# Gate rows and the rotary swap by transfers, the rotary products on GpSimd

## The chip, the cores and the metric

The kernel runs on one core of one Trainium2 chip. A core has TensorE (matrix products, PE in the profile), VectorE (DVE), ScalarE (ACT), GpSimd (POOL), SyncE (SP, which here only issues transfers) and 16 DMA engines. The metric is the time of one execution on the device in microseconds.

## The reference

Two blocks of two layers each run over 256 tokens of width 1024, in fp32. The first block takes its shifts, scales and gates from a vector `c` (adaLN): each of its four sublayers ends in `x + gate * y`. The second block begins with an attention that selects keys by an index score, and its queries, keys, index queries and index key get a rotary embedding.

```python
def first_block(x, c, ...):
    for i in range(DEPTH):
        mod = silu(c) @ ada_w[i] + ada_b[i]
        sh1, sc1, gt1, sh2, sc2, gt2 = jnp.split(mod, N_MOD, axis=-1)
        ...                                  # short convolution (i = 0) or RWKV-7 (i = 1)
        x = x + gt1[:, None, :] * y
        h = _modulate(_rmsnorm(x, norm_g[i, 1]), sh2, sc2)
        x = x + gt2[:, None, :] * (jnp.square(jax.nn.relu(h @ mlp_w1[i])) @ mlp_w2[i])
    return _rmsnorm(x, final_g)

def apply_rope(x):                           # per head of 64
    x1, x2 = x[..., :32], x[..., 32:]
    return jnp.concatenate([x1 * c - x2 * sn, x1 * sn + x2 * c], axis=-1)
```

## The kernel before

Every weight matrix is cut into units of 1 MB (256 columns of 1024 rows, or half of 512 columns). SyncE loads them in order into four `stage` buffers (`load_unit`, four units ahead). ScalarE makes the upper part `w_hi` of a unit, VectorE the rest `w_lo = stage - w_hi`, each in two halves (`split`), and TensorE multiplies three times (hi*hi, hi*lo, lo*hi) into a bank of PSUM (`unit`, `up_unit`, `wide_unit`). Each engine's program is written out by hand in its own order; semaphores tie them together. TensorE's order is the one that the others follow.

adaLN's modulation is summed piece by piece beside the convolution and the first MLP and ends as columns, `mods[layer][q, 8 * part + t]`, one value per partition. A gate is needed as a row, the same on all 128 partitions, since `y` is laid out with tokens on partitions. Before, `row_of_columns` (L2353) makes it on TensorE: eight products of a broadcast column with the identity, in two banks, and `row_copy` (L1039) on ScalarE copies both banks to `gate_rows[r]`. That happens four times: row 0 beside the convolution's unit 9, row 1 ahead of the first MLP's last wide units, row 2 in RWKV's output projection, row 3 behind it. Around row 3 TensorE also runs `unread`, a product of 512 columns that nobody reads, while VectorE computes the norm's scales. VectorE's `residual` (L1597 and following) multiplies by the row (L1611).

The rotary embedding goes in eight pieces: index key (128 channels), two of index queries, key, four of queries. For each, ScalarE copies the unit's bank to `rope_in` (`rope_load`, L1366); TensorE multiplies by a permutation matrix with signs (`rot`, L2781, `rot_query`, L2853), which swaps the halves of each head; VectorE multiplies the swapped one by `sin_root` (L2058); GpSimd multiplies the copy by `cos_root` (L850); VectorE adds them (L2060) and signals `rope_done`. `sin_root` and `cos_root` are the tables times the tokens' norm factors, made by VectorE (L2140, L2141). GpSimd takes the pieces strictly in order, each after the `rope_done` of the last, and between them makes the `w_lo` of three of the query units (L860). L2838 is the index scores, L2792 the logits of a pair of heads, L2803 and L2815 to L2819 the transposed shares and their products with the values. L1406 on ScalarE makes `k_dup`, the keys in both halves of the partitions.

The stage's order on TensorE is: units 0 and 1, `root_to_row`, then the swaps between units 2 to 8, with the index scores and the logits of the first pairs beside them.

Of the kernel before, what the change touches and what calls it, by code (L numbers as in the profile page):

```python
# [13 lines left out]
P = 128  # L14
SEQ = 256
# [33 lines left out]
CONST_PARTS = ((("ident", P), ("mean", P), ("ones", P), ("rot", P)),  # L49
# [13 lines left out]
def constant_table():  # L63
# [13 lines left out]
    rot = np.zeros((P, P))  # L77
    for m in range(P):
        d = m % HD
        rot[m + HD // 2 if d < HD // 2 else m - HD // 2, m] = -1.0 if d < HD // 2 else 1.0  # L80
    put("rot", rot)
# [11 lines left out]
    put("sin", np.tile(np.sin(ang), (4, 1)))  # L93
# [7 lines left out]
def build(nc, A, out):  # L101

    with ExitStack() as ctx:
# [65 lines left out]
        ident, mean_w, ones_w, head_ones, head_mean, rot_w = (c_(n) for n in ("ident", "mean", "ones", "head_ones", "head_mean", "rot"))  # L169
# [105 lines left out]
        rope_in = [at(f"rope_in{i}", [P, 2, SEQ], r_off[3] + 2048 * i) for i in range(2)]  # L275
        rope_c = at("rope_c", [P, 2, SEQ], r_off[3] + 4096)
# [285 lines left out]
        LAST_SET = ADA_SETS - 1  # L562

# [64 lines left out]
        def _(sp):  # L628
# [29 lines left out]

            for k in range(ADA_FIRST):
# [7 lines left out]
            for u in range(NU):  # L667
# [40 lines left out]
        row_done, row_out, out_made, final_made = (sem(n) for n in ("row_done", "row_out", "out_made", "final_made"))  # L708
# [18 lines left out]
        rot_done, rope_done, ki_copied, cos_done, kdup_ready = (sem(n) for n in ("rot_done", "rope_done", "ki_copied", "cos_done", "kdup_ready"))  # L727
# [9 lines left out]
        def _(pool):  # L737
# [135 lines left out]
        def _(act):  # L873
# [2161 lines left out]
```

## Time and profile before

| | us |
|---|---|
| median of 3 runs | 1352.4 (1350.19 to 1352.61) |
| profiled execution, its own time | 1350.53 |
| its span | 1348.8 |
| TensorE busy | 1303.3 |
| VectorE busy | 948.8 |
| ScalarE busy | 701.5 |
| GpSimd busy | 128.3 |

Times in the rows are microseconds from the start of the span. A product's record shows a modelled end that overlaps the next, so that the cost of one is read from start to start. An idle time in brackets is the engine's own just before, with what ended it. A releaser is inferred; where a wait has several semaphores, the name can be another's.

### The profile page before, as it was taken

The page shows a single profiled execution, that of the slowest core. Times are in us where ns is not written, and L with a number is a line of the kernel's source. Part 1 is how long each engine was busy: PE and PEld are TensorE (multiplying, and loading weights), DVE is VectorE, ACT ScalarE, POOL GpSimd, SP SyncE. Part 2 cuts the span into 40 slices and gives each one's busy share as a digit, 9 for nine tenths or more (in the row PEclk, how much of TensorE's full clock was granted, in tenths as well). Part 3 has the DMA queues.
Part 4 walks back from the last instruction along what each step waited for, and adds up shares of the span by engine and source line. Part 5 has one row for each costly group of instructions (what it writes and reads, how often), then busy time and mean ns, then how long its engine had stood idle before and what let it go on. Part 6 is the DMA issues. An engine that isn't in the chain of part 4 may idle for free. (4 is left out here: it accounts for less than half of the span.)

```text
span 1348.8 us, 24952 instructions
## 1 busy us (share of the span) xinstructions
PE 1303.3 (97%) x10507; PEld 1129.8 (84%) x10507; DVE 948.8 (70%) x1433; ACT 701.5 (52%) x1211; POOL 128.3 (10%) x133
## 2 busy tenths in 40 slices
PE   4999999999999999999999999999999999999997
PEld 2998888998899897788888887888888998888886
DVE  1887788976768776675566888666656677756655
ACT  2544544434567555564444648654445566644443
POOL 0000000010200764100000042000000021000000
PEclk9999999999999999999999999999999999999999
DMA  9996799995341012356665532465555543565561
GB/s 362 372 363 237 299 356 380 352 343 167 115 156 64 4 35 97 95 176 201 188 189 176 182 113 91 148 206 192 187 190 160 174 139 126 172 188 194 183 197 50
DMA packets 177575, 256.90 MB, mean 190 GB/s; under 512 B 10488, under 2 KB 122552, under 8 KB 177464
## 3 DMA queue, kind: packets, MB, share of 16 engines
q1 hardware_dynamic: 177464, 255.31, 56.8%
q8 instruction: 83, 1.36, 0.4%
q14 instruction: 28, 0.23, 0.1%
HBM read 254.25 MB, written 1.05 MB: 189 GB/s over the span
## 5 line engine op out<-in xcount | busy, mean ns | idle before, releaser
L1514 DVE TENSOR_TENSOR w_lo<-stage,w_hi 128x1024 fp32r<-128x1024 f32 (+1 forms) x372 | 447.6, 1239 | 160.4 <-ACT w_hi L889 160.0
L889 ACT ACTIVATE w_hi<-stage 128x1024 fp32r<-128x1024 f32 (+1 forms) x378 | 380.1, 1049 | 211.7 <-PE acc L2318 191.9
L2316 PE MATMUL acc<-w_hi,z_hi 128*128 128x512 f32 x640 | 252.6, 395 | 1.6 <-DVE z_lo L1963 1.6
L2318 PE MATMUL acc<-w_hi,z_lo 128*128 128x512 f32 x640 | 249.4, 390 | 0.0
L2317 PE MATMUL acc<-w_lo,z_hi 128*128 128x512 f32 x640 | 249.2, 389 | 0.0
L2259 PE MATMUL un<-h_both,w_hi 128*128 128x256 f32 x736 | 214.3, 291 | 1.8 <-POOL w_lo L860 1.1
L2260 PE MATMUL un<-h_both,w_hi 128*128 128x256 f32 x736 | 208.1, 283 | 0.0
L2261 PE MATMUL un<-h_both,w_lo 128*128 128x256 f32 x736 | 208.0, 283 | 0.0
L2259 PEld LDWEIGHTS un<-h_both,w_hi 128*128 128x128 f32 x736 | 140.8, 191 | 9.5 <-issue 5.4
L2316 PEld LDWEIGHTS acc<-w_hi,z_hi 128*128 128x128 f32 x640 | 120.1, 188 | 27.8 <-issue 4.0
L2260 PEld LDWEIGHTS un<-h_both,w_hi 128*128 128x128 f32 x736 | 141.0, 192 | 1.2 <-issue 0.7
L2318 PEld LDWEIGHTS acc<-w_hi,z_lo 128*128 128x128 f32 x640 | 120.1, 188 | 25.4
L2261 PEld LDWEIGHTS un<-h_both,w_lo 128*128 128x128 f32 x736 | 140.9, 191 | 0.0
L2317 PEld LDWEIGHTS acc<-w_lo,z_hi 128*128 128x128 f32 x640 | 120.3, 188 | 23.5
L2297 PE MATMUL un<-h_both,w_hi 128*128 128x512 f32 x384 | 121.2, 397 | 0.4 <-DVE w_lo L1514 0.4
L2297 PE MATMUL side<-h_both,w_hi 128*128 128x512 f32 x384 | 120.8, 396 | 0.4
L2300 PEld LDWEIGHTS side<-h_both,w_lo 128*128 128x128 f32 x384 | 72.1, 188 | 17.0
L2300 PEld LDWEIGHTS un<-h_both,w_lo 128*128 128x128 f32 x384 | 72.1, 188 | 16.9
L2300 PE MATMUL un<-h_both,w_lo 128*128 128x256 f32 x384 | 75.5, 278 | 0.0
L2300 PE MATMUL side<-h_both,w_lo 128*128 128x256 f32 x384 | 75.4, 278 | 0.0
L1796 DVE SCALAR_TENSOR_TENSOR ada_sum<-ada_buf,small,ada_sum 128x1024 f32<-128x1024 f32 x49 | 62.8, 1282 | 1.0
L2297 PEld LDWEIGHTS un<-h_both,w_hi 128*128 128x128 f32 x384 | 59.1, 189 | 1.6 <-DVE w_lo L1514 0.6
(393 smaller groups left out, 1886.0 us busy)
## 6 DMA issues: line engine op xcount, KB each, us to landing
stage<-in_mlp_w SPq DMA_DIRECT2D x64, 1024.0 KB
ada_buf<-in_ada_w SPq DMA_DIRECT2D x48, 1024.0 KB, 11.4
stage<-in_w_up SPq DMA_DIRECT2D x32, 1024.0 KB
stage<-in_w_down SPq DMA_DIRECT2D x32, 1024.0 KB
stage<-in_conv_w_in SPq DMA_DIRECT2D x12, 1024.0 KB
stage<-in_rw_w_rkv SPq DMA_DIRECT2D x12, 1024.0 KB
stage<-in_w_in_a SPq DMA_DIRECT2D x8, 1024.0 KB
stage<-in_w_kv_b SPq DMA_DIRECT2D x8, 1024.0 KB
```

What stands on the lines that cost most here:

```text
L889: A_(w_hi[u % 2][:, half, 0:n], stage[u % NSTAGE][:, half, 0:n], ACT.Copy).then_inc(hi_made, 1)
L1514: V.tensor_tensor(w_lo[u % 2][:, half, 0:n], stage[u % NSTAGE][:, half, 0:n], w_hi[u % 2][:, half, 0:n].bitcast(F32), ALU.subtract).then_i ...
L1796: V.scalar_tensor_tensor(out=to[:], in0=rows, scalar=by, in1=to[:], op0=ALU.mult, op1=ALU.add).then_inc(ada_weighed, 1)
L2259: MM(out, hi_l, hi_r, start=start, stop=False, skip_group_check=True)
L2260: MM(out, hi_l, lo_r, start=False, stop=False, skip_group_check=True)
L2261: return MM(out, lo_l, hi_r, start=False, stop=stop, skip_group_check=True)
L2297: MM(pair[:, m, :, :], wh[:, kt, c], h_both[:, kt, :, :], start=(kt == 0), stop=False, skip_group_check=True)
L2300: ins = MM(pair[:, m, 0, :], wl[:, kt, c], h_hi[:, kt, :], start=False, stop=(kt == KT - 1), skip_group_check=True)
L2316: MM(y, z_hi[:, kt, q], wh[:, i, :], start=(first and kt == 0), stop=False, skip_group_check=True)
L2317: MM(y, z_hi[:, kt, q], wl[:, i, :], start=False, stop=False, skip_group_check=True)
L2318: ins = MM(y, z_lo[:, kt, q], wh[:, i, :], start=False, stop=(last and kt == KT - 1), skip_group_check=True)
```

## The change

Gate rows: `row_of_columns` and `row_copy` are gone with their waits. SyncE writes the gate's columns to a buffer in memory (`keep_gate`) as soon as its order reaches unit 14, 32, 41 or 60, and reads them back as a row broadcast over the partitions (`spread_gate`) at unit 15, 33, 66 and, for the last, 68. `residual` waits for that transfer. In place of the fourth row's products TensorE runs four more `unread`s.

Rotary embedding: the swap matrix is gone, and its signs go into the sine table. ScalarE waits for its own copy to `rope_in` and issues four transfers, each of 32 partitions of `rope_in` to the neighbouring 32 of `rope_turned`. GpSimd multiplies by the cosine, waits for the four transfers, multiplies by the sine. VectorE only adds. TensorE's eight products are gone, and with them its waits for `rope_done` ahead of units 7 and 8.

```diff
-CONST_PARTS = ((("ident", P), ("mean", P), ("ones", P), ("rot", P)),
+CONST_PARTS = ((("ident", P), ("mean", P), ("ones", P), ("still", P)),
...
-    put("sin", np.tile(np.sin(ang), (4, 1)))
+    put("sin", np.tile(np.sin(ang), (4, 1)) * np.where(i % HD < HD // 2, -1.0, 1.0)[:, None])
...
         rope_in = [at(f"rope_in{i}", [P, 2, SEQ], r_off[3] + 2048 * i) for i in range(2)]
+        rope_turned = [at(f"rope_turned{i}", [P, 2, SEQ], tmp_off + 4096 + 2048 * i) for i in range(2)]
         rope_c = at("rope_c", [P, 2, SEQ], r_off[3] + 4096)
...
+        GATE_SETS = (2, 5, 8, 11)
+        KEEP_GATE_AT = (14, 32, 41, U_RWO)
+        SPREAD_GATE_AT = (15, 33, U_RWO + 6)
...
+            def keep_gate(r):
+
+                sp.wait_ge(ada_added, ADA_ORDER.index(GATE_SETS[r]) + 1)
+                c0 = 8 * (GATE_SETS[r] % 6)
+                sp.dma_start(gate_kept[r].rearrange("(t q) -> q t", q=P), mods[GATE_SETS[r] // 6][:, c0:c0 + KT],
+                             allow_slow_non_contiguous=True).then_inc(sem("gate_written"), 16)
+
+            def spread_gate(r):
+
+                sp.wait_ge(sem("gate_written"), 16 * (r + 1))
+                sp.dma_start(gate_rows[r][:], gate_kept[r].unsqueeze(0).to_broadcast([P, D])).then_inc(sem("gate_spread"), 16)
+
...
                     sp.dma_start(final_row[:], row_of(VEC_FINAL)).then_inc(sem("final_row_in"), 16)
+                    spread_gate(3)
...
+                if u in KEEP_GATE_AT:
+                    keep_gate(KEEP_GATE_AT.index(u))
+                if u in SPREAD_GATE_AT:
+                    if u == U_RWO + 6:
+                        sp.wait_ge(sem("bonus_gated"), len(GN_GROUPS))
+                    spread_gate(SPREAD_GATE_AT.index(u))
                 load_unit(u)
...
                 pool.wait_ge(un_free, freed(V_A + ROPE_USE[r]))
                 if r:
                     pool.wait_ge(sem("rope_done"), r)
-                G.tensor_tensor(rope_c[:, 0:n, :], rope_in[r % 2][:, 0:n, :], cos_root.unsqueeze(1).to_broadcast([P, n, SEQ]), ALU.mult)\
-                    .then_inc(sem("cos_done"), 1)
+                G.tensor_tensor(rope_c[:, 0:n, :], rope_in[r % 2][:, 0:n, :], cos_root.unsqueeze(1).to_broadcast([P, n, SEQ]), ALU.mult)
+                pool.wait_ge(sem(f"rope_landed{r % 2}"), 64 * (r // 2 + 1))
+                turned = rope_turned[r % 2][:, 0:n, :]
+                G.tensor_tensor(turned, turned, sin_root.unsqueeze(1).to_broadcast([P, n, SEQ]), ALU.mult).then_inc(sem("cos_done"), 1)
 
                 if r in (ROPE_K, ROPE_Q, ROPE_Q + 1):
...
-            def row_copy(r, low, high):
-
-                act.wait_ge(row_done, r + 1)
-                A_(gate_rows[r][:, 0:HALF], flat(low), ACT.Copy)
-                A_(gate_rows[r][:, HALF:D], flat(high), ACT.Copy).then_inc(row_out, 1)
-
...
                 copy_set(COPIED_AT.get(S_CONV + j))
-                if j == 9:
-                    row_copy(0, acc[0], acc[1])
...
             rw_split(3)
-            row_copy(2, stat_ps, misc)
             last_splits(U_RWO, N_MLP1)
             norm_split(N_MLP1, gain[:, 3, :], mods[1][:, 24:32], U_MLP[1] + 1)
-            row_copy(3, stat_ps, misc)
             mlp(1, N_A, vecT[:, VEC_GA:VEC_GA + KT])
 
...
                 if r >= 2:
                     act.wait_ge(rope_done, r - 1)
                 A_(rope_in[r % 2][:, 0:n, :], un[v % 2][:, 0:n, :], ACT.Copy, scale=scale).then_inc(un_free, 1)
+                act.wait_ge(un_free, freed(v))
+                for g in range(4):
+                    to, src = 32 * g, 32 * (g ^ 1)
+                    act.dma_start(rope_turned[r % 2][to:to + 32, 0:n, :], rope_in[r % 2][src:src + 32, 0:n, :]).then_inc(sem(f"rope_landed{r % 2}"), 16)
...
-                    dve.wait_ge(row_out, row + 1)
+                    dve.wait_ge(gate_spread, 16 * (row + 1))
                     link(V.tensor_tensor(g[:, k % 2, :], y, gate_rows[row][:, HALF * h:HALF * (h + 1)], ALU.mult))
                     y = g[:, k % 2, :]
...
-            def rope(r, n, dst, bank=misc):
-                dve.wait_ge(rot_done, r + 1)
-                link(V.tensor_tensor(dst, bank[:, 0:n, :], bc4(sin_root, n), ALU.mult))
+            def rope(r, n, dst):
                 dve.wait_ge(cos_done, r + 1)
-                V.tensor_tensor(dst, dst, rope_c[:, 0:n, :], ALU.add).then_inc(rope_done, 1)
+                V.tensor_tensor(dst, rope_turned[r % 2][:, 0:n, :], rope_c[:, 0:n, :], ALU.add).then_inc(rope_done, 1)
 
...
-            dve.wait_ge(rot_done, ROPE_KI + 1)
+            dve.wait_ge(wi_turned, 1)
...
-                rope(ROPE_Q + j, 2, q_fm[:, 2 * j:2 * j + 2, :], un[(V_A + 5 + j) % 2])
+                rope(ROPE_Q + j, 2, q_fm[:, 2 * j:2 * j + 2, :])
 
             rope_query(0)
             select(rounds - rounds // 2)
-            V.tensor_scalar(sel_bias[:], score[:], 0.5 * TAKEN, NEG, ALU.is_gt, ALU.mult).then_inc(sem("keys_chosen"), 1)
-            dve.wait_ge(sem("keys_chosen"), 1)
...
-            def row_of_columns(r, columns, low, high):
-
-                for t in range(KT):
-                    ins = MM(flat((low, high)[t // 4])[:, P * (t % 4):P * (t % 4) + P], columns[:, t:t + 1].to_broadcast([P, P]), ident,
-                             start=True, stop=True)
-                ins.then_inc(row_done, 1)
-
...
-                if tiles[0] == 0 and n == N_A:
-                    pe.wait_ge(row_out, 4)
...
-                            if m == 1 and g == 0 and j == 1:
-                                pe.wait_ge(row_out, 4)
                             up_unit(u + 2 * UPD * g + j, up_pair[j % 2], ready)
-                    if m == 0 and g == GROUPS - 1:
-                        pe.wait_ge(ada_added, LAST_SET)
-                        row_of_columns(1, mods[0][:, 40:48], stat_ps, misc)
                     if g == GROUPS - 1:
                         last_units(u + 2 * UPD * g + UPD, z_ready(zc + UPD * g), first=False, turn={1: N_A, 2: N_B}.get(m))
                         continue
...
-                if j == 9:
-                    pe.wait_ge(ada_added, 3)
-                    row_of_columns(0, mods[0][:, 16:24], acc[0], acc[1])
-            pe.wait_ge(row_out, 1)
             last_units(U_CONV_OUT, z_ready(Z_CONV))
...
-            row_of_columns(2, mods[1][:, 16:24], stat_ps, misc)
             wide_unit(U_RWO + 2, 1, rwo_ready, rows=range(0, 2))
             wide_unit(U_RWO + 2, 1, rwo_ready, rows=range(2, 4))
             wide_unit(U_RWO + 3, 3)
             keep_warm(V_MLP[1], 1)
-            pe.wait_ge(row_out, 3)
-            row_of_columns(3, mods[1][:, 40:48], stat_ps, misc)
-            unread(un[V_MLP[1] % 2], 2)
+            unread(un[V_MLP[1] % 2], 6)
             turn_first(N_MLP1)
...
-            def rot(r, n, v):
-                pe.wait_ge(un_free, freed(v))
-                if r:
-                    pe.wait_ge(rope_done, r)
-                MM(misc[:, 0:n, :], rot_w, rope_in[r % 2][:, 0:n, :], start=True, stop=True).then_inc(rot_done, 1)
...
-                if k >= 7:
-                    pe.wait_ge(rope_done, ROPE_Q + k - 6)
...
-            def rot_query(j):
-                v = V_A + 5 + j
-                pe.wait_ge(un_free, freed(v))
-                MM(un[v % 2][:], rot_w, rope_in[(ROPE_Q + j) % 2][:], start=True, stop=True).then_inc(rot_done, 1)
...
-                nc.tensor.transpose(misc[:, 1, IDX_HEADS * a:IDX_HEADS * (a + 1)], rope_in[ROPE_KI % 2][HD:KI_COLS, 0, P * a:P * a + P],
+                ins = nc.tensor.transpose(misc[:, 1, IDX_HEADS * a:IDX_HEADS * (a + 1)], rope_in[ROPE_KI % 2][HD:KI_COLS, 0, P * a:P * a + P],
                                     ident[HD:KI_COLS, HD:KI_COLS])
-            rot(ROPE_KI, 1, V_A)
+            ins.then_inc(wi_turned, 1)
             a_unit(2)
-            rot(ROPE_QI, 2, V_A + 1)
             a_half(3, 0)
-            rot(ROPE_QI + 1, 2, V_A + 2)
             a_half(3, 1)
             index_scores(0)
             a_half(4, 0, tokens=True)
-            rot(ROPE_K, 2, V_A + 3)
             index_scores(1)
             a_half(4, 1, tokens=True)
             a_unit(5)
-            rot_query(0)
             a_unit(6)
             pe.wait_ge(kdup_ready, KV_HEADS)
             pe.wait_ge(score_relu, QT * IDX_HEADS // 2)
             a_products(0)
             a_half(7, 0)
-            rot_query(1)
             a_products(1)
             a_half(7, 1)
             z_of = z_ready(Z_A)
...
                 if p == 1:
                     a_half(8, 0)
...
-                if p in (1, 3):
-                    rot_query(p // 2 + 2)
```

## Rows read from the trace of the kernel before

**Rows 1.** The page, busy time of each engine, share of span and instructions

```profile
PE 1303.3 (97%) x10507; PEld 1129.8 (84%) x10507; DVE 948.8 (70%) x1433; ACT 701.5 (52%) x1211; POOL 128.3 (10%) x133
```

**Rows 2.** Table by stretches: length, busy PE, PEld, DVE, ACT, POOL, granted clock, DMA

```profile
133.00:330.00 197.00, 196.31 (x1312) 173.14 (x1311) 158.31 (x171) 93.09 (x129) 6.29 (x3) 1.00 0.90 323
755.00:830.00 75.00, 71.17 (x562) 61.61 (x563) 63.64 (x149) 45.44 (x107) 27.64 (x32) 1.00 0.41 130
```

**Rows 3.** Timeline of PE around row 0 (start, length, what), and all of L2356

```profile
96.67 2.05 PE L2356 MATMUL acc<-const,mod 128*128 128x128 f32 x16
98.48 0.36 PE L2259 MATMUL un<-h_both,w_hi 128*128 128x256 f32 x1
...
L2356 PE MATMUL side<-const,mod x48: 270/275/275, 308.9 to 569.3; 128*128 128x128 f32 x48
```

**Rows 4.** Timeline of PE around row 2

```profile
552.38 1.95 PE L2356 MATMUL side<-const,mod 128*128 128x128 f32 x16
555.74 0.47 PE L2316 MATMUL acc<-w_hi,z_hi 128*128 128x512 f32 x1 [1.42 <-DVE z_lo L1963]
```

**Rows 5.** Timeline of PE around row 3 and the unread products

```profile
566.75 1.02 PE L2363 MATMUL un<-const 128*128 128x512 f32 x2
567.60 1.95 PE L2356 MATMUL side<-const,mod 128*128 128x128 f32 x16
569.38 1.88 PE L2363 MATMUL un<-const 128*128 128x512 f32 x4
571.55 1.09 PE L2326 MATMUL acc<-const,xs_sq 128*128 128x128 f32 x8 [0.29 <-DVE xs_sq L1537]
```

**Rows 6.** Issues by line: ns of an issue (min/median/max), us to landing

```profile
L681 SPq DMA_DIRECT2D lora_g2b<-in_rw_g x4: 417/421/429, 335.9 to 337.3; - x4
DMA to landing us min/median/max: 3.9/4.1/4.4
...
L672 SPq DMA_DIRECT2D lora<-in_rw_a x1: 4837/4837/4837, 163.3 to 163.3; - x1
...
DMA to landing us min/median/max: 2.0/2.1/2.1
```

The first landing line is L681's (32 KB each, behind other loads), the second L701's (the output, 256 KB each, nothing else in flight).

**Rows 7.** Timeline of SP's queue at units 14 and 15

```profile
97.46 0.39 SPq L644 DMA_DIRECT2D stage<-in_conv_w_out  x1
...
104.15 0.39 SPq L644 DMA_DIRECT2D stage<-in_conv_w_out  x1
```

**Rows 8.** Timeline of ACT in the rotary stage

```profile
763.23 1.99 ACT L889 ACTIVATE w_hi<-stage 128x1024 fp32r<-128x1024 f32 x2
...
825.69 0.58 ACT L1366 ACTIVATE rope_in<-un 128x512 f32<-128x512 f32 x1
```

**Rows 9.** Timeline of PE in the rotary stage

```profile
765.78 0.35 PE L2259 MATMUL un<-h_both,w_hi 128*128 128x256 f32 x1 [0.18 <-ACT rope_in L1366]
...
779.15 1.16 PE L2838 MATMUL acc<-ki_fm,qi_fm 64*128 64x128 f32 x16
...
828.96 0.93 PE L2792 MATMUL un<-k_dup,q_fm 64*128 64x128 f32 x8 [0.43 <-DVE q_fm L2060]
```

**Rows 10.** Timeline of DVE in the rotary stage

```profile
764.41 4.64 DVE L1514 TENSOR_TENSOR w_lo<-stage,w_hi 128x1024 fp32r<-128x1024 f32 x4 [0.42 <-ACT w_hi L889]
768.97 0.41 DVE L2140 TENSOR_TENSOR rstd<-const,acc 128x256 f32<-128x256 f32 x1
...
774.01 3.43 DVE L1514 TENSOR_TENSOR w_lo<-stage,w_hi 128x1024 fp32r<-128x1024 f32 x2
...
778.08 0.69 DVE L2060 TENSOR_TENSOR qi_fm<-qi_fm,rope_c 128x512 f32<-128x512 f32 x1
```

**Rows 11.** Timeline of POOL in the rotary stage

```profile
769.85 0.75 POOL L850 TENSOR_TENSOR rope_c<-rope_in,rstd 128x256 f32<-128x256 f32 x1 [219.98 <-DVE rstd L2141]
771.27 1.28 POOL L850 TENSOR_TENSOR rope_c<-rope_in,rstd 128x512 f32<-128x512 f32 x1 [0.67 <-DVE ki_fm L2060]
774.23 2.12 POOL L850 TENSOR_TENSOR rope_c<-rope_in,rstd 128x512 f32<-128x512 f32 x1 [1.68 <-DVE qi_fm L2060]
```

More of the change, by code:

```diff
@@ L76, in constant_table @@
     put("head_mean", same_head / HD)
[L77 to L81, printed above, removed]
     s, q = i[:, None] % CHUNK, np.arange(CHUNK)[None, :]
@@ L98, in constant_table, with build @@
     return t
-def build(nc, A, out):
+def build(nc, A, out, gate_kept):
     with ExitStack() as ctx:
@@ L167, in c_ @@
             return const[i][:, lo - CONST_AT[i]:hi - CONST_AT[i]]
-        ident, mean_w, ones_w, head_ones, head_mean, rot_w = (c_(n) for n in ("ident", "mean", "ones", "head_ones", "head_mean", "rot"))
+        ident, mean_w, ones_w, head_ones, head_mean = (c_(n) for n in ("ident", "mean", "ones", "head_ones", "head_mean"))
         level_t = c_("level_t").rearrange("p (j q) -> p j q", j=6)
@@ L707, in build @@
         xs_low_made, xs_high_made, turned, first_done = (sem(n) for n in ("xs_low_made", "xs_high_made", "turned", "first_done"))
-        row_done, row_out, out_made, final_made = (sem(n) for n in ("row_done", "row_out", "out_made", "final_made"))
+        gate_written, gate_spread, out_made, final_made = (sem(n) for n in ("gate_written", "gate_spread", "out_made", "final_made"))
         scaled_made, sq_f_ready, both_ready, square_ready, root_row_done, root_row_out, tables_made = (
@@ L726, in build @@
                              "bonus_gated", "weighed", "scaled", "group_done", "last_done"))
-        rot_done, rope_done, ki_copied, cos_done, kdup_ready = (sem(n) for n in ("rot_done", "rope_done", "ki_copied", "cos_done", "kdup_ready"))
+        wi_turned, rope_done, ki_copied, cos_done, kdup_ready = (sem(n) for n in ("wi_turned", "rope_done", "ki_copied", "cos_done", "kdup_ready"))
         score_done, score_relu, score_used = sem("score_done"), sem("score_relu"), sem("score_used")
@@ L1070, in mlp @@
                             split_half(uu + 2, 1)
-                            if m == 0 and g == GROUPS - 1:
-                                row_copy(1, stat_ps, misc)
                         if m == 0:
@@ L2158, in rope_query @@
             def rope_query(j):
-                rope(ROPE_Q + j, 2, q_fm[:, 2 * j:2 * j + 2, :], un[(V_A + 5 + j) % 2])
+                rope(ROPE_Q + j, 2, q_fm[:, 2 * j:2 * j + 2, :])
             rope_query(0)
             select(rounds - rounds // 2)
-            V.tensor_scalar(sel_bias[:], score[:], 0.5 * TAKEN, NEG, ALU.is_gt, ALU.mult).then_inc(sem("keys_chosen"), 1)
-            dve.wait_ge(sem("keys_chosen"), 1)
+            link(V.tensor_scalar(sel_bias[:], score[:], 0.5 * TAKEN, NEG, ALU.is_gt, ALU.mult))
             pair_logits(0, 0)
@@ L2478, in mlp @@
                                 free_bank(v + UPD * g + j)
-                            if m == 1 and g == 0 and j == 1:
-                                pe.wait_ge(row_out, 4)
                             up_unit(u + 2 * UPD * g + j, up_pair[j % 2], ready)
-                    if m == 0 and g == GROUPS - 1:
-                        pe.wait_ge(ada_added, LAST_SET)
-                        row_of_columns(1, mods[0][:, 40:48], stat_ps, misc)
                     if g == GROUPS - 1:
@@ L2521, in _ @@
             mlp(0, N_MLP0)
-            pe.wait_ge(row_out, 2)
             free_bank(V_RKV + 1)
@@ L3030 @@
     arrays["in_vec_table"] = np.concatenate([np.reshape(inputs[n], (-1, P)) for n in VECTORS])
+    gate_kept = nc.dram_tensor("gate_kept", (4, D), F32, kind="Internal").ap()
     aps = {n[3:]: nc.dram_tensor(n, a.shape, mybir.dt.from_np(a.dtype), kind="ExternalInput").ap() for n, a in arrays.items()}
     out = nc.dram_tensor("out_x", (1, SEQ, D), F32, kind="ExternalOutput").ap()
-    build(nc, aps, out)
+    build(nc, aps, out, gate_kept)
     return run_bass_kernel_spmd(nc, [arrays], core_ids=[0]).results[0]["out_x"]
```

2 lines of the change are left out of this document (removed).

## The prediction

> **What bounds the kernel now.** I read the page first: TensorE is busy for 1303.3 of 1348.8 us, VectorE for 70%, ScalarE for 52% [rows 1]. The table by stretches then says where there is any room: from 133 to 330 us TensorE works for 196.31 of 197 us, so an instruction taken off it there is time gained, while from 755 to 830 us, the first attention block with its rotary embedding, it works for 71.17 of 75 us and waits for others several times [rows 2]. The granted clock is 1.00 in both, the upper of its two levels, 2.4 GHz, so the clock plays no part. The timelines of each engine around the nine places that the diff touches are the third view: they show what ends each wait.
>
> The profiled execution took 1350.53 us (span 1348.8), 0.1% under the median of 1352.4. The sum is made in its terms and its difference added to the median.
>
> **Gate rows 0 and 1.** `row_of_columns` is eight small products, sixteen records. For row 0 the sixteen start at 96.67 and the next unit starts at 98.48: 1.81 us of TensorE. Row 1's products are of the same form and length, 0.275 us each, overlapped [rows 3]; I take 1.7 us. Both stand in stretches without idle time, and the units behind them have their weights and banks ready, so both arrive in full: **-3.5 us**. The two copies of each row on ScalarE go too; it waits there, so they are worth nothing.
>
> **Gate row 2.** Its products start at 552.38. The next product starts only at 555.74, and 1.42 us of that is idle, ended by VectorE's `z_lo` [rows 4]. That chain (group norm, `rw_split`) does not contain the row, so TensorE reaches the same wait 1.7 us earlier: **0**.
>
> **Gate row 3 and the filler.** Before: one `unread` (566.75 to 567.60, 0.85 us), the row's products (1.78 us), two `unread`s (from 569.38, 1.7 us), then turned tiles from 571.55, where TensorE had idled 0.29 us for VectorE's `xs_sq` [rows 5]. After: 1 + 6 `unread`s, 7 x 0.855 = 6.0 us from 566.75, to 572.75. The tiles were ready at 571.55 and now wait for the filler: **+1.2 us**. ScalarE loses two copies behind `norm_split`; at most 0.3 us comes back, I take **-0.3**.
>
> **The gate rows by transfer.** SyncE issues four writes of 128 x 8 single elements to memory and four broadcasts of 512 KB. The nearest rows: a load of 1024 short runs held SyncE for 4.84 us behind a full queue; small ones take 0.42 us [rows 6]. Each `keep_gate` waits for a set that was added several units before, and each `spread_gate` follows a whole load later: load 14 is issued at 97.46 and load 15 at 104.15 [rows 7], 6 us for a write to come back. Behind a waiting SyncE stand the next weight load and adaLN pieces, which are issued four units ahead, over 15 us. I cost them at nothing; if a write took over 15 us, TensorE would wait for weights by the excess. Row 2's broadcast can be issued when GpSimd has gated the last group, long before VectorE needs it.
>
> **The rotary stage, removed.** Eight swap products, one of half size. They have the form of an `unread`, 0.855 us [rows 5]: 7 x 0.855 + 0.43 = 6.4 us of TensorE. VectorE loses eight products of 0.69 us; it isn't the bound.
>
> **The rotary stage, added.** Each `rope_load` on ScalarE now waits for its own copy and then issues four transfers. No row shows an issue by ScalarE. The nearest are SyncE's four transfers of 32 partitions, 0.42 us each, started 0.47 us apart [rows 6]: 4 x 0.47 = **1.9 us** in which ScalarE computes nothing, eight times. The bounds are 0.1 us (the sequencer hands them off) and 2.2 us. I take 1.9. A transfer lands 2.0 us after its issue in the quiet case, 4.1 behind others [rows 6]; from the end of the copy to data landed is then 0.1 + 3 x 0.47 + 2.0 = 3.5 us. GpSimd then needs a second product of 1.28 us, behind its first.
>
> Walk through the stage, times of before on the left:
> - ScalarE's `w_hi` at 763.23 [rows 8] stands behind the first four issues: 765.2. TensorE's unit at 765.78 [rows 9] needs it through VectorE, so it starts at 767.8: **+2.0**, and the 0.43 us of the removed swap are lost in that wait.
> - The second four issues stand before the next `w_hi`. VectorE's four `w_lo` (764.41, 4.64 us) end 4.2 us later, and with them the sine and cosine tables of 768.97 [rows 10]: 773.2 to 773.9.
> - GpSimd starts on the tables. Its three embeddings are a chain, since each waits for the sum of the last: 773.9 + 2 x 0.75 + 0.43 + 2 x 1.28 + 0.69 + 2 x 1.28 + 0.69 (products from [rows 11], the sums of VectorE of 0.69) + some six hand-overs of 0.1 = 783; a `w_lo` pair that VectorE does between them ran 3.43 us beside GpSimd [rows 10] and makes it 784. Before, the last of these sums was done at 778.08 + 0.69 = 778.77, and TensorE's index scores, L2838, started at 779.15 [rows 9, 10]. Now: **+4.9**.
> - The swap behind it is gone (-0.9). After that the same happens for the queries: `k_dup` stands behind four issues, GpSimd's `w_lo` splits for three units stand behind cos, landing, sin and sum. Each loses about 1 us and each removed swap gives 0.86 back: TensorE stays **+4 to +5** up to 821.
> - The last query's load (825.69 [rows 8]) comes 5.5 us later: 4 of it TensorE's own, 1.5 from the issues in ScalarE's queue. Copy 0.6, landed 3.5, sine 1.3, sum 0.8: done at 837.4, where TensorE took it at 828.96 after a wait of 0.43 us [rows 9]. **+8.5.**
> I take +8 for the stage. After 829 TensorE runs without gaps, so nothing gives it back.
>
> **Sum.** -3.5 + 0 + 1.2 - 0.3 + 8 = **+5.4 us**: 1355.9 in the terms of the profile, **1357.8 us** as a median (+0.4%).
>
> **Rivals.**
> *Faster: the swaps' time arrives.* If ScalarE issues at next to nothing, transfers land within 1.5 us, and the chain over GpSimd has slack, TensorE gains 3.5 + 6.4 - 0.9 = 9.0: 1343.4 us. For it: TensorE is 97% busy. Against it: L2838 had 0.4 us of slack, and the last query none [rows 9]. Half of it would be 1348.
>
> *No change: the issues are cheap, the chain isn't.* With 0.1 us for the issues the first two steps vanish. The last query then needs 0.6 (copy) + 2.1 (landed) + 1.28 + 0.1 + 0.69 = 4.8 us from 825.69, where it took 3.2; of these 1.6 us some 1.1 come back, since TensorE reaches its load earlier by the swaps that are gone: +0.5. -2.6 + 0.5 = -2.1: 1350.3 us.
>
> *Later still: the shared port.* VectorE's `w_lo` pair took 3.43 us, where two pairs in a row take 4.64 [rows 10], beside a GpSimd product of 2.12 us instead of 1.28 [rows 11]. With twice the GpSimd products this can hit three more places by 1 us each: 1361. It decides only if their starts coincide.
> The Trainium skill ("SBUF — State Buffer", section on the two separate sides) says more: a GpSimd operation and a VectorE operation with two SBUF inputs exclude each other for the whole instruction. By this rule each of the eight added products could hold VectorE for 1.28 us, at most 10 us; where its `w_lo` runs, the row agrees in kind.
>
> *Not slower, for another reason: ScalarE had the time.* It idles 75 - 45.4 = 30 us in this stage [rows 2], so the issues might fit. That is the no-change case again; it fails where `w_hi` follows `rope_load` directly.
>
> **Chances.** The forecast (net +2.7 or more, with the port) 0.63; no change 0.22; faster 0.15. A measurement tells about 0.2%, 2.7 us, from no change, and these are the bounds of the three. The range leaves out the faster half of the third case and what lies above two port collisions: 1349 to 1361.
>
> **What would show it.** Right: ScalarE's issues at about 0.47 us each; `w_hi` after the first `rope_load` about 2 us later against that copy; TensorE waiting for VectorE before the index scores; the longest wait before the logits of the sixth pair. The stretch from 580 to 750 unchanged in length, row 2's place still ended by `z_lo`, and the turned tiles after seven fillers starting 6 us behind the last product. Wrong: issues of 0.1 us; TensorE waiting for weights after a `spread_gate`; VectorE waiting for a gate row; or a stage from 763 to 829 that is shorter than before.

## The result, and where the time went

The changed kernel takes **1375.4 us** (median; 1373.8 to 1380.1) against 1352.2 of the kernel before: 23 us between the medians; the ratio is 1.0185, 95% interval 1.0163 to 1.0206, or +22 to +28 us. The direction was predicted. The size was not: 1357.8, with a range up to 1361. The profiled execution took 1373.79 us (span 1372.0), 23.3 more than that of before. The page has TensorE no busier than in [rows 1], so nothing was added to it; it waits:

```profile
PE 1301.9 (95%) x10435; PEld 1129.3 (82%) x10435; DVE 944.4 (69%) x1425; ACT 698.2 (51%) x1203; POOL 138.2 (10%) x141
```

To see where, I set the n-th `w_hi` of ScalarE in one trace beside the n-th in the other, and took the difference of their starts, in us. The kernels of the experiments below are in the same table. A difference that stays from one row to the next is a stretch of unchanged length.

```
start in   changed  g1     g5     g6     g3       r1     r6     r3     r7
before     kernel   gate   again  form   turned   rot    unread noiss. dve
  85.2     -0.7    -0.8    0.0   -0.9    0.4      0.4   -0.5    0.0   -0.4
 120.1     -1.2    -1.2    1.0   -2.2   -1.0      0.4   -0.5    0.0   -0.4
 279.7     -1.2    -1.1    1.0   -2.2   -1.0      0.4   -0.5    0.0   -0.4
 316.4      1.9     2.5    4.7   -4.0   -2.8      0.4   -0.5   -0.1   -0.4
 352.5      1.9     2.5    4.7   -4.0   -2.8      0.4   -0.5    0.0   -0.4
 362.4      3.6     2.5    4.7   -2.3   -2.8      2.0   -0.5    1.6   -0.4
 552.6      3.5     3.8    4.7   -0.1   -2.7      2.0   -0.4    1.5   -0.3
 564.9      5.1     3.8    4.7   -0.1   -2.7      1.9   -0.4    1.5   -0.3
 587.8      5.9     4.6    4.3   -0.5   -2.7      1.9   -0.4    1.5   -0.3
 753.5      5.9     4.6    4.3   -0.5   -2.7      1.9   -0.4    1.5   -0.3
 783.0     13.4     4.5    4.2   -0.2   -2.5     10.3    8.0    3.5   -0.7
 820.7     15.5     4.6    4.3   -0.1   -2.4     16.3    9.4    3.5   -0.6
 845.6     22.2     4.6    4.3   -0.1   -2.4     23.4   14.3    5.9    1.2
1325.3     22.1     4.6    4.3   -0.1   -2.4     23.4   14.5    5.9    1.1
```

The changed kernel loses in four places: 3.1 us around gate row 1 (280 to 316), 1.7 at the start of RWKV (352 to 362), 2.3 at rows 2 and 3 (553 to 588), 16.3 in the rotary stage (753 to 846). Row 0 gives 0.5. From 588 to 753 and from 846 to 1325 nothing changes; the last 1.1 us of the difference come behind 1325.

**The gate writes.** The issue line of the changed kernel (ns of an issue min/median/max, then us to landing):

```profile
L662 SPq DMA_DIRECT2D gate_kept<-mod x4: 367/612/1648, 90.5 to 404.3; - x4
DMA to landing us min/median/max: 11.8/13.8/17.8
```

Its timeline of SyncE's queue at the write of row 1:

```profile
208.10 0.37 SPq L662 DMA_DIRECT2D gate_kept<-mod  x1
212.40 3.77 SPq L643 DMA_DIRECT2D stage<-in_mlp_w  x1
225.93 0.34 SPq L668 DMA_DIRECT2D gate_row<-gate_kept  x1
226.31 0.46 SPq L643 DMA_DIRECT2D stage<-in_mlp_w  x1
```

A write is cheap to issue and takes 12 to 18 us to land. From 216.2 to 225.9 SyncE stood and waited for it, with the loads behind. The third write, row 2's, stands in the same queue at 267 us, ahead of another load and another piece of adaLN's weights:

```profile
267.42 0.85 SPq L662 DMA_DIRECT2D gate_kept<-mod  x1
268.31 4.18 SPq L643 DMA_DIRECT2D stage<-in_mlp_w  x1
272.53 9.93 SPq L653 DMA_DIRECT2D ada_buf<-in_ada_w  x1
```

What the write of row 0 does to the transfers behind it is seen in the table by stretches (columns as in [rows 2]; the last two are the DMA share and GB/s), of the kernel before:

```profile
96.00:104.00 8.00, 8.00 (x72) 7.49 (x71) 7.86 (x13) 3.88 (x6) 0.00 (x0) 1.00 0.80 303
```

and of the changed kernel:

```profile
96.00:104.00 8.00, 7.77 (x84) 6.90 (x80) 7.86 (x14) 4.40 (x6) 0.00 (x0) 1.00 0.48 91
```

91 GB/s instead of 303: the 4 KB write holds up what is queued behind it. (It does so even where SyncE doesn't wait for it: `g2_late` below reads the row back later, and the same 8 us have 90 GB/s.) Of row 0's 1.8 us TensorE loses 0.79 again at 112 us, waiting for the transfer of `ada_buf`; near 290 us it is this wait. VectorE's timeline and TensorE's:

```profile
289.54 2.60 DVE L1808 SCALAR_TENSOR_TENSOR ada_sum<-ada_buf,small,ada_sum 128x1024 f32<-128x1024 f32 x2 [7.59 <-DMA ada_buf<-in_ada_w]
292.20 0.64 PE L2443 MATMUL side<-ada_sum,const 128*32 128x256 f32 x8 [2.62 <-DVE ada_sum L1808]
```

Two writes stand ahead of it, not one. I compared the landing of each piece of adaLN's weights with that of the same piece before. From row 1's write to 262 us the pieces land some 8 us late, and TensorE does not idle. The piece at hand, the first behind row 2's write, was issued at 272.53 and landed 17.0 us later, 11.3 us late, where the one ahead of it was 6.2 late. In between, from 276 to 284 us, the rate is 77 GB/s against 378 before. No run takes row 2's write away alone, so its share is read from the trace and not shown by an experiment.

**The granted clock.** Stretches of the changed kernel in which it fell; in the profile of before it is 1.00 in every stretch but the last 10 us:

```profile
292.00:296.00 4.00, 3.02 (x19) 2.56 (x20) 3.97 (x5) 2.01 (x2) 2.98 (x2) 0.68 1.05 366
340.00:346.00 6.00, 5.00 (x21) 3.83 (x20) 5.75 (x15) 1.52 (x4) 2.30 (x3) 0.72 0.78 248
558.00:564.00 6.00, 4.73 (x14) 3.81 (x15) 4.00 (x5) 0.80 (x2) 0.00 (x0) 0.72 0.54 164
...
776.00:780.00 4.00, 4.00 (x27) 4.00 (x27) 2.01 (x2) 2.01 (x2) 0.00 (x0) 0.73 0.88 267
790.00:796.00 6.00, 4.05 (x28) 3.86 (x29) 3.21 (x6) 1.04 (x3) 1.63 (x3) 0.72 0.76 212
846.00:854.00 8.00, 5.54 (x32) 4.04 (x30) 3.94 (x9) 3.50 (x14) 1.26 (x1) 0.57 0.02 5
```

Each stands behind idle time of TensorE, and each has part of its length at the lower of the two levels, 1.2 GHz. A single fall, as at 340, 558 and 790 us, is 6 us x (1 - 0.72) = 1.7 us of clock; the stretches at 292 and 776 us hold only a part of one, the last line holds two. What the `w_hi` behind the fall lose against before is 1.65 us for the one at 341 us, where the waits are those of before, and 1.6 us for the one at row 2. The Trainium skill, "TensorE: Matmul & The Clock Gate" (Part 1), calls the lower level the default that activity releases; the rows agree, in these stretches the clock is back once products run.

**The rotary stage.** The changed kernel's timeline of ScalarE at the first load:

```profile
768.84 0.37 ACT L1374 ACTIVATE rope_in<-un 128x256 f32<-128x256 f32 x1
769.24 2.50 ACTq L1378 DMA_DIRECT2D rope_turned<-rope_in  x4
771.84 2.00 ACT L909 ACTIVATE w_hi<-stage 128x1024 fp32r<-128x1024 f32 x2 [2.63 <-issue]
```

The line of its issues:

```profile
L1378 ACTq DMA_DIRECT2D rope_turned<-rope_in x32: 514/612/627, 769.2 to 843.7; - x32
DMA to landing us min/median/max: 1.9/2.0/5.6
```

The timeline of TensorE, and of GpSimd, where they wait longest in the stage:

```profile
774.40 0.35 PE L2268 MATMUL un<-h_both,w_hi 128*128 128x256 f32 x1 [3.56 <-ACT rope_in L1374]
791.95 2.08 PE L2817 MATMUL acc<-ki_fm,qi_fm 64*128 64x128 f32 x16 [4.32 <-DVE qi_fm L2070]
845.83 0.44 PE L2796 MATMUL acc<-pair_turned,vA_tok 128*64 128x128 f32 x4 [4.12 <-ACT pair_turned L1362]
847.30 1.26 POOL L871 TENSOR_TENSOR rope_turned<-rope_turned,rstd 128x512 f32<-128x512 f32 x1 [4.01 <-DMA rope_turned<-rope_in]
849.35 1.66 PE L2773 MATMUL un<-k_dup,q_fm 64*128 64x128 f32 x8 [2.46 <-DVE q_fm L2070]
```

They answer to [rows 8, 9, 11]. Four issues hold ScalarE for 2.5 us; behind the last four stands `pair_turned`, and TensorE waits 4.12 us for it.

### The profile page after: what moved, and what is told of

Same layout as the page of the kernel before. It is cut to its first block, busy times and chain, and to the rows that moved or that the text cites. A ratio compares the mean times of both kernels' runs of the same rounds, so it can differ in the third digit from the quotient of the medians.

```text
span 1372.0 us, 24828 instructions
## 1 busy us (share of the span) xinstructions
PE 1301.9 (95%) x10435; PEld 1129.3 (82%) x10435; DVE 944.4 (69%) x1425; ACT 698.2 (51%) x1203; POOL 138.2 (10%) x141
## 4 chain that ended last, share of the span: by engine, by line
PE 76%; DVE 10%; DMA 6%; ACT 3%; issue 2%; POOL 1%; ACTq 1%; SPq 0%; DVEq 0%; POOLq 0%
PE acc L2325 10%; PE acc L2327 9%; PE acc L2326 9%; PE side L2306 7%; PE un L2306 6%; PE un L2268 5%; PE un L2269 5%; PE un L2270 5%; DMA ada_buf<-in_ada_w 4%; PE side L2309 3%; PE un L2309 3%; DVE w_lo L1526 3%; PE acc L2639 3%; PE side L2639 2%; DMA gate_kept<-mod 1%
```

## The experiments

Each kernel is compared with the kernel before on the same chip; the ratio has its 95% interval. Four sets ran on four chips.

**One part at a time.** `g1_gate` has the gate part of the diff alone, `r1_rot` the rotary part alone.

> Only the gate rows by transfer; the rotary stage as before. In the profiled run of the changed kernel the lead over the kernel before stood at +5.9 us from 600 to 750 us, ahead of the rotary stage. Theory 'two separate parts': this kernel is 5 to 7 us slower than before (1357.5 to 1359.5 us), with the steps at the same places: TensorE idle for VectorE's ada_sum near 290 us, then for z_lo near 557 us, and the granted clock at its lower level for some 3 us after each. Rival 'one cause': a lower clock or slower transfers over the whole run, brought in by the rotary stage's load, make both; then this kernel is within 2 us of before.

> Only the rotary swap by transfers; gate rows as before. Theory 'two separate parts': 15 to 18 us slower than before (1367 to 1370 us), since the stage from 763 to 850 us lengthened by 16.3 us. The four transfers of a load hold ScalarE for 2.5 us (0.61 us each), and the granted clock is at its lower level after the idle times of TensorE of 3.6, 4.3 and 4.1 us. Rival 'one cause': the delay of the gate part shifts loads against the stage and makes part of it; then it is under 12 us.

g1_gate: 1355.9 us, 1.0027 (1.0013 to 1.0041). r1_rot: 1374.0 us, 1.0166 (1.0150 to 1.0181). Two separate parts, though both sizes missed what was expected, the gate part on the low side and the rotary part, at 22 us against 15 to 18, on the high side: +3.7 and +22.4 make 26, within the 22 to 28 us of the whole's interval. The gate part scatters: ten executions from 1350.3 us (granted clock 0.999) to 1359.7 (0.992). The kernel before goes with its clock too: 1349.8 at 0.999, 1353.2 at 0.996. In r1_rot the stage costs 21.4 us where the whole has 16.3; its clock fell for 13.7 us of clock there, against 6.8 in the changed kernel.

One more part of g1_gate's expectation failed. At row 2 TensorE idled for `z_lo` as long as in the changed kernel, but its clock did not fall, and the units behind it lost nothing (the table has 3.8 and 3.8). The wait, and the stretch of the same 6 us:

```profile
559.53 0.47 PE L2326 MATMUL acc<-w_hi,z_hi 128*128 128x512 f32 x1 [3.20 <-DVE z_lo L1973]
558.00:564.00 6.00, 4.47 (x20) 3.71 (x21) 4.22 (x6) 1.06 (x2) 0.00 (x0) 1.00 0.53 170
```

**The rotary part taken apart.** From the bottom up. `r3_noissue` and `r7_dve` have no transfer at all:

```diff
-                for g in range(4):
-                    act.dma_start(rope_turned...
-                pool.wait_ge(sem(f"rope_landed{r % 2}"), 64 * (r // 2 + 1))
-                G.tensor_tensor(turned, turned, sin_root...
+                G.tensor_tensor(turned, rope_in[r % 2][:, 0:n, :], sin_root...     # r3_noissue
+                link(V.tensor_tensor(dst, rope_in[r % 2][:, 0:n, :], bc4(sin_root, n), ALU.mult))   # r7_dve
```

`r6_unread` has r3_noissue's products and r1_rot's issues, to another place:

```diff
-                    act.dma_start(rope_turned[r % 2][to:to + 32, 0:n, :], rope_in...
+                    act.dma_start(rope_dump[r % 2][to:to + 32, 0:n, :], rope_in...
```

> r3_noissue (1355.5 us: no swap at all, both products on GpSimd) with the sine product back on VectorE, as in the kernel before; the halves are still not swapped (that part of the computation is left out). Theory 'GpSimd's second product': it is what kept r3_noissue 3.7 us above the kernel before although TensorE has 6.4 us less to do; here the time falls to 1345 to 1348 us, below before. Rival 'the swaps were fillers': without them TensorE only waits longer and its clock falls, whoever multiplies; then 1352 us or more.

> The rotary part alone without its 32 transfers: GpSimd multiplies rope_in itself by the sine, so the halves are not swapped (that part of the computation is left out) while every product and sum stays. Theory 'issues and landing': without them the stage has TensorE's 6.4 us less and only the second product of 1.28 us on its chain; 1346 to 1351 us, at or below before. Rival 'GpSimd': its second products, beside VectorE's, are what lengthens the stage; then it stays over 1360 us.

> The rotary part alone with its 32 transfers issued by ScalarE as in r1_rot, but to a place that nobody reads: GpSimd multiplies rope_in by the sine and waits for no landing (the halves are not swapped, that part of the computation is left out). It differs from r3_noissue (1355.5 us) by the issues alone, from r1_rot (1374.0 us) by the landing alone. Theory 'issues on ScalarE': at least 11 of the 18.6 us, 1366 us or more. Rival 'landing': within 5 us of r3_noissue.

r7_dve: 1352.2 us, 1.0008 (0.9999 to 1.0018). r3_noissue: 1355.5, 1.0030 (1.0020 to 1.0039). r6_unread: 1365.6, 1.0111 (1.0096 to 1.0127). With r1_rot these are steps of one cause each (difference of the ratios, times 1352 us; from the intervals, the lower three are uncertain by some 2, 2.5 and 3 us). r3_noissue fits neither of its two theories, which asked for at most 1351 or over 1360.

| | from | us |
|---|---|---|
| eight swaps off TensorE | r7 - before | +1.1 (-0.1 to +2.4) |
| sine product to GpSimd | r3 - r7 | +3.0 |
| 32 issues by ScalarE | r6 - r3 | +11 |
| the wait for their landing | r1 - r6 | +7.4 |

The first step is the surprise: 6.4 us fewer products on TensorE, and no time gained. That is what the rival of r7_dve had said (1352 us or more, longer waits and a fall of the clock). Its trace says why. Its `w_hi` at 803 us comes 1.8 us early; behind that TensorE waits for others (its timeline):

```profile
802.64 0.36 PE L2255 MATMUL un<-h_both,w_hi 128*128 128x256 f32 x1 [1.37 <-POOL w_lo L856]
811.24 0.93 PE L2782 MATMUL acc<-k_dup,q_fm 64*128 64x128 f32 x8 [1.57 <-DVE pair_logit L2072]
813.21 0.36 PE L2255 MATMUL un<-h_both,w_hi 128*128 128x256 f32 x1 [1.05 <-POOL w_lo L856]
827.22 0.44 PE L2805 MATMUL acc<-pair_turned,vA_tok 128*64 128x128 f32 x4 [2.02 <-ACT pair_turned L1350]
828.53 1.55 PE L2782 MATMUL un<-k_dup,q_fm 64*128 64x128 f32 x8 [0.43 <-DVE q_fm L2057]
```

The second half of the stage is set by the key selection, the softmax and GpSimd's `w_lo`; this last row starts 0.4 us ahead of its place before [rows 9], but runs at the lower clock, for a fall from 828.7 to 832.1 us: the lead of 0.6 us at 821 has become 1.2 us of loss at 846. Both issue and landing theories of r6_unread hold in part: 11 of the 18.5 us are issues, 0.4 short of the 1366 us that the first asked for.

**Other issuers, and fillers.** Both start from r1_rot:

```diff
-                    act.dma_start(rope_turned...                   # r4_sp
+                load_unit(u)
+                if u - 5 - U_KI in ROPE_USE:
+                    sp.wait_ge(un_free, freed(V_A + ROPE_USE[r]))
+                        sp.dma_start(rope_turned...                # four, as before
...
+            keep_warm(V_A + 2, 4)                                  # r5_warm
             a_unit(2)
...
+            unread(acc[3], 5)
             index_scores(0)
```

> The rotary part alone (r1_rot, 1374.0 us), but SyncE issues the 32 transfers, each four behind a load that comes later than the copy they wait for; ScalarE issues none. Theory 'issues on ScalarE': the 2.5 us that each four hold ScalarE are most of the 18.6 us between r1_rot and r3_noissue, so this kernel takes 1357 to 1363 us. Rival 'landing': the time from the copy to data landed is what counts, and behind the weight loads in SyncE's queue it gets longer; then 1368 us or more.

> r1_rot with four products that nobody reads ahead of the third unit and five ahead of the first index scores, where TensorE idled 3.6 and 4.3 us and the granted clock then stood at its lower level (0.50) for some 3.4 us each. The idle times and what they wait for stay. Theory 'the idle time brings the clock down': the clock stays at 1.00 at both places and the kernel is 2 to 4 us faster than r1_rot (1370 to 1372). Rival 'the clock falls by itself or costs nothing beside the waits': within 1 us of r1_rot, or slower, since the fillers can be late.

r4_sp: 1379.8 us, 1.0213 (1.0199 to 1.0227), slower still. ScalarE is free, but in SyncE's queue the transfers land after 4.5 us instead of 2.1 (medians), behind 1 MB loads, and GpSimd waited six times for them, 25.5 us in all; in r1_rot three times, 10.2 us. The line of its issues shows that one costs SyncE nearly what it costs ScalarE:

```profile
L695 SPq DMA_DIRECT2D rope_turned<-rope_in x32: 507/590/1847, 765.2 to 851.4; - x32
```

r5_warm: 1374.0 us, 1.0174 (1.0159 to 1.0188), no gain over r1_rot that is clear of the spread (by the ratios at most some 2 us, where 2 to 4 were expected). The fillers did keep the clock. The stretch in r1_rot:

```profile
768.00:778.00 10.00, 6.70 (x37) 6.73 (x38) 5.43 (x7) 4.49 (x5) 0.00 (x0) 0.66 0.47 136
```

and in r5_warm:

```profile
768.00:778.00 10.00, 9.49 (x69) 8.22 (x68) 5.75 (x8) 4.26 (x5) 0.93 (x2) 1.00 0.53 143
```

but the index scores wait for the same chain of ScalarE, VectorE and GpSimd: they start at 788.02 us, in r1_rot at 789.11, and 0.7 us of that lead was there at 753. So 5.1 us of clock given back bring 0.4 us at the index scores, and the table's row at 783 us (8.6, less the 1.2 of 753, against 10.3 less 1.9 in r1_rot) 1.0. A lower clock costs time where TensorE is what sets the pace behind it, as at 352 and 558 us, and little in the first half of this stage. My rule of 1.7 us for each fall is refuted for it.

**The gate writes.** `g2_late` is g1_gate with rows 0 and 1 read back later. `g3_turned` keeps rows 2 and 3 on TensorE, as before, and changes the write of rows 0 and 1:

```diff
-        SPREAD_GATE_AT = (15, 33, U_RWO + 6)                       # g2_late
+        SPREAD_GATE_AT = (17, 37, U_RWO + 6)
...
+        SPREAD_GATE_AT = (16, 34)                                  # g3_turned
+                    V.transpose(gate_turned[s // 5][:, :], mods[0][:, 16:48])      # in 32 x 32 blocks, after the set is added
...
+                for b in range(4):
+                    sp.dma_start(gate_kept[r].rearrange("(t b q) -> b t q", b=4, q=32)[b], m[32 * b + lo:32 * b + lo + KT, :])
```

> The gate part alone as in g1_gate, but the rows 0 and 1 are read back later: at SyncE's units 17 and 37 instead of 15 and 33, so that SyncE never waits for a write (they took 11.8 to 17.8 us to land). Theory 'SyncE waits': the loads behind it are on time, the 2.6 us idle for ada_sum near 290 us and the clock's fall behind it go, and the kernel is 3 to 5 us faster than g1_gate (1353 to 1355). Rival 'the write itself': its 1024 elements hold the DMA queue, so that the transfers behind it are late whoever waits; then it is within 1.5 us of g1_gate.

> The kernel before with gate rows 0 and 1 alone made by transfers; rows 2 and 3 stay on TensorE, and the rotary stage as before. VectorE turns the gate's columns by one 32 x 32 block transpose each, so that a row is written in 32 runs of 128 bytes and not in 1024 single elements; it is read back two units later. Theory 'the write's form and its wait were the cost': the 3.5 us of TensorE's products arrive, 1347 to 1349.5 us against 1351.7 before. Rival 'any filler is needed': TensorE meets a wait that the products had covered; then 1351 us or more.

g2_late: 1353.4 us, 1.0013 (1.0004 to 1.0022), 2.5 below g1_gate by the medians and 1.9 by the ratios, whose intervals overlap; it lies in the range expected. SyncE's wait is a part, then, of a size that is barely clear of the spread; 90 GB/s from 96 to 104 us and a wait of 0.80 us for `ada_sum` remain. Row 2's write stands at 267 us in this kernel too. g3_turned: **1347.8 us, 0.9978 (0.9969 to 0.9987)**, faster than the kernel before by 3.5 us, what two rows cost TensorE. The table has it: -1.4 at row 0, -1.8 at row 1.

**The fillers at rows 2 and 3, and the chip.** `g5_fill` is g2_late with

```diff
             output_rows(4)
+            unread(stat_ps, 2)
...
-            unread(un[V_MLP[1] % 2], 6)
+            unread(un[V_MLP[1] % 2], 4)
```

> g2_late (1353.4 us) with two products that nobody reads where row 2's products stood, ahead of the wait for z_lo, and four instead of six behind row 3's place. In g2_late TensorE idled 3.19 us for z_lo (1.42 before), the granted clock then fell, and the units behind it came 1.6 us later; the six fillers then ran 1.1 us longer than the wait that they cover. Theory 'row 2's products kept the clock up': no fall near 555 us, the step of 1.6 us gone, and the 1.1 us with it, so 1350.7 to 1351.5 us. Rival 'the fall comes by itself': the step of 1.6 us stays and only the 1.1 us go, 1352.3 us.

g5_fill: 1355.9 us, 1.0029 (1.0018 to 1.0041), slower than g2_late although its trace has both steps gone. At 316 us it stood at +7.7 in the terms of the table, g2_late at -1.5, in code that is the same. So four kernels were run on one chip: g2_late and g5_fill again, g3_turned again, and `g6_form`, g5_fill with the writes of g3_turned for all four rows. (g6_form also writes row 2 at unit 60 and not at 41, and reads rows 0 and 1 back at units 16 and 34 and not 17 and 37.)

> The kernel of g2_late once more, beside the three below on one chip. Theory 'the cost of the element writes differs from chip to chip': it comes out as g5_fill did over its own part up to 300 us, some 6 us later there than g2_late, or as g2_late did; whichever it is, g5_again lies below it. Rival 'g5_fill's own edits made it slower': g5_again lies above this one by 2 us or more, as g5_fill (1355.9) lay above g2_late (1353.4).

> The kernel of g5_fill once more. Its trace showed the two steps gone (row 2's 1.6 us, the fillers' 1.1 us) and 6 us more up to 300 us, where its code is that of g2_late. Theory 'chip': on the same chip as g2_again it is 1 to 3 us faster than that one. Rival 'own edits': slower than g2_again by 2 us.

> g5_again with one thing changed, the form of the writes: VectorE turns each gate's columns by a block transpose, and a row is written in 32 runs of 128 bytes, not in 1024 single elements (rows 0 and 1 are then read back at units 16 and 34, rows 2 and 3 both written at unit 60). All four rows by transfer. Theory 'the write's form': the loads behind it are on time, 1346.5 to 1349 us, 4 us or more below g5_again. Rival 'any transfer put into SyncE's order there makes the later ones late': above 1350 us.

> The kernel of g3_turned once more (rows 0 and 1 by 128-byte runs, rows 2 and 3 on TensorE), on the same chip as the others. Expected 3 to 4 us below the kernel before, as there (1347.8 against 1351.3), and within 1 us of g6_form, whose rows 2 and 3 are replaced by fillers of the same length.

| | us | ratio | 95% |
|---|---|---|---|
| g2_again | 1358.9 | 1.0054 | 1.0037 to 1.0071 |
| g5_again | 1354.8 | 1.0033 | 1.0022 to 1.0044 |
| g6_form | 1350.1 | 0.9994 | 0.9985 to 1.0004 |
| g3_again | 1348.1 | 0.9982 | 0.9973 to 0.9992 |

The same kernel with element writes took 1353.4 us on one chip and 1358.9 on another, where before took 1351.7 and 1350.4: the price of such writes differs from chip to chip, or from one occasion to the next, which one set on each chip can't tell apart. Fillers: -4.1 us by the medians, -2.8 by the ratios. In the traces 2.8 of it stand at their places (g2_again goes from 4.7 at 553 us to 7.1 at 588, g5_again from 4.7 to 4.3); 1.5 are a fall of the clock at 821 us in g2_again, far behind them.

Form of the writes: -4.7 us. Its effect alone shows at row 0, where only the form and a later read-back differ (the rates above, 90 GB/s and 312); near 290 us it is mixed with row 2's write, which in g6_form and in g3_turned no longer stands at 267 us.

What the two extra products at row 2 do: g2_again waits 3.21 us for z_lo, g5_again 1.49, and behind that stand, in g2_again,

```profile
560.00:566.00 6.00, 5.55 (x17) 4.44 (x18) 3.18 (x4) 0.36 (x1) 0.00 (x0) 0.72 0.55 158
```

and in g5_again:

```profile
560.00:566.00 6.00, 5.58 (x25) 4.63 (x26) 3.15 (x4) 0.33 (x1) 0.00 (x0) 1.00 0.54 161
```

g3_again came 2.3 us below the kernel before, where 3 to 4 were expected. g6_form missed its range (up to 1349) by 1.1 us and lies 2 above g3_again, not within 1; its profile has falls of the clock at 336 and 462 us that cost 1.7 and 2.0 us. The transfers of rows 2 and 3 are not needed for either: the first is there in r1_rot, r3_noissue and r4_sp, the second in g3_again (1.3 us) and r5_warm, which make both rows on TensorE. Whether they make such falls more frequent stays open.

## Why the prediction was wrong

By its own steps, in the profiled execution:

| step | said | was |
|---|---|---|
| gate row 0 | -1.8 | -0.5 |
| gate row 1 | -1.7 | +3.1 |
| RWKV's start | 0 | +1.7 |
| gate row 2 | 0 | +1.6 |
| row 3 and the fillers | +0.9 | +0.8 |
| rotary stage | +8 | +16.3 |

The steps said add up to 5.4 us, those measured to 23.0 of the 23.2 by which the span grew.

**The write was costed at nothing.** I took the 6 us between two loads [rows 7] as enough, from the landings of 2 to 4 us of [rows 6]. It took 12 to 18. I had named the point from which it would hurt ("over 15 us") and gave the weights and the adaLN pieces the same slack of four units. Near 290 us neither had it. ScalarE waited 6.41 us for a weight load (its `w_hi` at 286.9 us), VectorE 7.59 us for an adaLN piece; TensorE's longest wait, 2.62 us, was the one for the adaLN piece, and 0.79 us more went to the `w_lo` behind. By the trace two writes made the piece late: the pieces had not caught up with row 1's when row 2's came. The row at hand was L672's: its 1024 short runs held SyncE for 4.84 us, and I read it as the queue being full. A rule I did not weigh: the Trainium skill, "DMA: Bandwidth & Descriptors" (Rules for kernel authors), says that a non-contiguous last dimension becomes one descriptor per element, and to rearrange; g6_form against g5_again gives 4.7 us for doing so here, with row 2's write moved as well.

**"The clock plays no part."** That was read from 1.00 in before, and it is the step that failed for row 2 and RWKV's start. Row 2's products hid no wait, as I said, and yet were worth 1.6 us in the profiled execution: with them TensorE idled 1.42 us [rows 4], without them 3.20, and the products behind ran at 1.2 GHz. That is not certain in each execution. Of the four traces without products there (the changed kernel, g1_gate, g2_late, g2_again), all idle 3.2 us, and three have the fall; none of the twelve with products or fillers there has it. At RWKV's start even the waits are those of before; the fall is there in five of the sixteen traces and not in the others, so that here the same waits end either way, and the 1.7 us there are this execution's and not the change's: r1_rot, r3_noissue and r4_sp have them with the gate rows as before. These runs don't tell what decides it.

**Row 3** was right: seven fillers end 6.0 us behind their start (571.84 to 577.85), past the ready tiles, and five (g5_again) take that back.

**The rotary stage** had the right mechanism and terms too small. The page's shift of 5.9 us taken off: first unit +2.8 (said +2.0), the tables at 780.26 +5.4 (+4.2), index scores +6.9 (+4.9), the sixth pair's logits +14.5 (+8.5), and 1.8 more at the lower clock behind them. An issue costs ScalarE 0.61 us and not the 0.47 that I took from SyncE's row, so four take 2.5 and not 1.9. The step that failed is the choice of the row, not the engine: for the same transfers SyncE took 0.59 us in r4_sp, while those of [rows 6] come from memory and not from another tile. By the equal clocks that the Trainium skill gives the two sequencers ("Advanced Engine Details and Errata", Clock Domains) an issue costs both the same, and with the same transfer the rows agree within 4%.

From the last copy's end (841.80) to GpSimd's product (847.30) are 5.5 us, not 3.5: 2.5 of issues and 3.0 of landing. And I let each removed swap give its 0.86 us back; r7_dve shows that none of it comes back (+1.1 us, not -6.4; without its one fall of the clock some 0.6 us would), so that credit of some 5 us over the stage was wrong, and the *faster* rival had no ground. The sum took +8 where my own walk ended at +8.5. The forecast's port rival fares better: GpSimd's second products cost 3.0 us, as much as it was priced at, and one beside VectorE's `w_lo` took 2.28 us. The single records there look like turns: VectorE's first subtraction ends at 789.00, GpSimd's product at 790.12, VectorE's second subtraction, which alone takes 1.2 us, at 791.20. Whether the port or their plain length on the chain makes the 3.0 these runs don't separate.

## What to carry over

Before a stage's time on the busiest engine is counted as gain, ask in each part of it who ends its waits: products that go from a stretch in which others set the pace give nothing, and products that stood ahead of a wait may have kept the clock up. One trace shows one outcome of the clock; look whether a step is there in the other traces before it is put down to the change. Cost a transfer by its runs and by what is queued behind it, adaLN pieces as well as weights, and turn columns into rows on chip before they are written. An issue costs the engine that makes it, here some 0.6 us on ScalarE and on SyncE alike, whatever else it has to do; take its price from a row of the same kind of transfer.

## What the runs showed of the hardware

A write of 4 KB in 1024 elements lands after 12 to 18 us and takes the DMA rate behind it from 303 to 91 GB/s for 8 us; from 85 to 316 us g2_late gains 1.0 us where the two rows give 3.6, so that the element writes cost it 2.5 us; reckoned so, the same code costs 8 to 11 us in the traces of g2_again, g5_again and g5_fill, on two other chips. In 32 runs of 128 bytes it costs nothing that is seen: from 96 to 104 us g6_form moved 312 GB/s. Small transfers from ScalarE's own queue landed in 2.1 us beside the weight loads, in SyncE's in 4.5 (medians). And the granted clock is not the same in two executions of one program. Each fall is 1.7 us of clock, of which 1.2 to 1.7 are seen in the time where TensorE sets the pace, and in g1_gate's ten executions time and clock go together: 9.5 us from the fastest to the slowest, 0.999 to 0.992.
